# Two transformer blocks on one core: both ends of the kernel rebuilt

## The chip, the cores and the metric

The kernel runs on 1 core of one Trainium2 chip. The metric is the device time of one execution in microseconds (us). Three runs of the kernel before gave 2267.41, 2269.45 and 2269.79 us; the median is 2269.45 us. All numbers below are from these runs and from one execution of the same kernel taken by the profiler.

## The reference

Two blocks follow each other on 256 tokens of width 2048, all in float32. What matters here is how the computation begins and how it ends:

```python
mem_n = rms_norm(mem, norm_mem_g)                    # mem: 256 x 2048
mkv = mem_n @ w_mem_kv                               # 2048 x 2048: the first products of the kernel
h = rms_norm(x, norm_in_g); proj = h @ w_in          # and so on: three kinds of attention, gates, w_out
...                                                  # second block: LRU, retention, w_out_2
u = rmsnorm(h, ln2_w)
ff = silu(u @ w_ffn_gate) * (u @ w_ffn_up)           # d_ff = 5632
h = h + ff @ w_ffn_down                              # 5632 x 2048: the last products
return rmsnorm(h, final_norm_w)                      # a mean over the whole row, then a scale
```

The last norm needs the sum of squares of a token's whole row of 2048 numbers before any number of that row can be written.

## The kernel before

**Weights.** Each product of 256 tokens with a weight is cut into tiles of 512 output columns and each tile into chunks of 256 rows of the weight (`per` = 2 blocks of 128), 512 KB each. A chunk is loaded by SyncE's (SP's) queue into one of four slots of `raw`. ScalarE (ACT, `split`, L509) rounds it to `w_hi`, VectorE (DVE, `split`, L743) makes the rest `w_lo` = raw - `w_hi`. A float32 product is three products of such parts: for each block of 128 rows and each of the two token halves `t`, TensorE (PE) does hi x hi (L1283), hi x lo (L1284) and lo x hi (L1285). A chunk is 2 x 2 x 3 = 12 matmuls. The first weight, `w_mem_kv`, has 8 chunks in a tile; the last, `w_ffn_down`, has 22. The tokens' side must be ready in both parts too (`memT_hi`, `memT_lo`).

**Order.** ACT, DVE and PE each run a list written out by hand: in `run(tile)` they go through the tile's chunks, and behind chunk `h` they do what hooks say. ACT and DVE work strictly in this order, so a hook that waits holds back the `split` of the next chunk.

**The start.** SP loads `ident` and the vectors (L430 to L432), then the first quarter of `mem`, the first chunk of weight, and the other quarters and chunks in turn; then, behind the first tile, the tables (704 KB) and `x` (two loads of 1 MB). PE turns the vectors (L1321, L1322) into `cols`. A quarter q of `mem` is turned by `job(q)`: 8 transposes on PE (L1150), 4 copies with a factor on ACT (`job_hi`, L540), 4 operations on DVE (`job_lo`, L780). PE does job(0) and job(1) before chunk 0, job(2) behind chunk 0 and job(3) behind chunk 1. ACT and DVE do job 0 first, job 1 behind their split of chunk 0, job 2 behind that of chunk 2, job 3 behind that of chunk 3. Chunks 2q and 2q+1 need job q.

**The end.** The last tile of `w_ffn_down` closes columns 1536 to 2047. Then DVE adds both token halves (L949), ACT squares both (L526), DVE multiplies both by the norm's weight (L1046), sums up (L773), makes the mean (L750); GpSimd (POOL) takes the power -0.5 (L461); DVE scales half 0 (L1137) and ACT scales half 1 (L725), each in two pieces of 1024 columns; SP stores four pieces of 512 KB (L450) and waits for them.

Of the kernel before, what the change touches and what calls it, by code (L numbers as in the profile page):

```python
# [112 lines left out]
def build(nc, x, mem, w_in, w_mkv, w_pa, w_pb, w_pm, w_out, fin1_g, w_in2, w_out2, w_gate, w_up, w_down,  # L113
          fin2_g, gate_a, gate_x, vecs, consts_d, decay_d, spill, out):
    ctx = ExitStack()
    with ctx:
# [100 lines left out]
        def bank(b, lo=0, hi=NW):  # L217
# [26 lines left out]
            sem(n) for n in ("in_const", "in_vec", "in_res", "in_g1", "in_dec", "in_gw", "in_g2"))  # L244
        spilled, in_h2, stored = sem("spilled"), sem("in_h2"), sem("stored")
        x_added = sem("x_added")
        pool_c, vec_ps, cols_ready, lam_abs, lam_e, lam_ready = (
            sem(n) for n in ("pool_c", "vec_ps", "cols_ready", "lam_abs", "lam_e", "lam_ready"))

# [154 lines left out]
        @block.sync  # L404
        def _(sp):
            w = Walk()

            def load(tile, then={}):
                per = tile.get("per", 2)
                src = tile["w"].rearrange("(c p) n -> p c n", p=P)  # L410
                if w.loop:
                    sp.to_reg(tile["col"] * 4)
                for h in chunks(tile):
                    s = w.n["g"] % SLOTS
                    sp.wait_ge(lo_ready, w("g", 1))
# [18 lines left out]
            first, *rest = tiles_memkv()  # L434
            load(first, {0: lambda: load_mem(1), 1: lambda: load_mem(2), 2: lambda: load_mem(3)})
            sp.dma_start(consts[:, C_ID + P:], consts_d[:, C_ID + P:]).then_inc(in_tables, 16)
            for t in range(NT):
                sp.dma_start(x_tok[:, t], x[t * P:(t + 1) * P, :]).then_inc(in_x[t], 16)
            load_all(rest + tiles_attention() + tiles_merge(0))
            w.rounds(sp, NG - 1, lambda i: load_all(tiles_merge(i + 1)))  # L440
            w.rounds(sp, NG // 2, lambda i: load_all(res_tiles(w_out, "m", None, i)))
            load_all(tiles_two())
            load_all(tiles_out2())
            w.rounds(sp, NF, lambda i: load_all(tiles_ffn(i)))
            w.rounds(sp, NG // 2, lambda i: load_all(res_tiles(w_down, "ff", None, i, FC // 2)))
            for t in range(NT):
                for m in range(2):
                    sp.wait_ge(out_made[t], m + 1)
                    c = slice(m * D // 2, (m + 1) * D // 2)
                    sp.dma_start(out[t * P:(t + 1) * P, c], h2[:, t, c]).then_inc(stored, 16)  # L450
            sp.wait_ge(stored, 32 * NT)


        @block.gpsimd
        def _(pool):
            nc.gpsimd.memset(mneg_c[:, :], -0.5).then_inc(pool_c, 1)
            pool.wait_ge(pool_c, 1)

            def norm_root(k, dst):
                pool.wait_ge(n_mean, k + 1)  # L460
# [36 lines left out]
            norm_root(5, R["out"]["r"])  # L497


        @block.scalar  # L500
        def _(act):
# [181 lines left out]
            def log_sigmoid_exp():  # L683
# [7 lines left out]
            four[1]["act_hooks"] = {7: [lambda: squares(x_tok, sumsq_x, lambda t: act.wait_ge(in_x[t], 16))]}  # L691
# [27 lines left out]
            act.wait_ge(x_added, 1)  # L719
            tile_squares(prev)  # L720
            act.wait_ge(out_scaled, NG)
            act.wait_ge(n_root, 6)
            for m in range(2):
                c = slice(m * D // 2, (m + 1) * D // 2)
                nc.scalar.activation(h2[:, 1, c], h2[:, 1, c], ACT.Copy, scale=R["out"]["r"][:, 1:2]).then_inc(out_made[1], 1)  # L725


        @block.vector
        def _(dve):
# [349 lines left out]
            def last_factors(name, k):  # L1079
# [11 lines left out]
            four[0]["dve_hooks"] = {0: jobs(memT_hi, memT_lo, V_MEM, 1), 2: jobs(memT_hi, memT_lo, V_MEM, 2),  # L1091
                                    3: jobs(memT_hi, memT_lo, V_MEM, 3), 7: [mem_factors]}
# [4 lines left out]
            job_lo(0, memT_hi, memT_lo, cols[:, V_MEM:V_MEM + KC])  # L1097
            prev = chain(four, None)
            log_sigmoid()
            tiles = tiles_attention()  # L1100
# [32 lines left out]
            sum_up(sums_a[:, :, :])
            root(sum_ab, 5)
            for m in range(2):
                c = slice(m * D // 2, (m + 1) * D // 2)
                nc.vector.tensor_scalar(h2[:, 0, c], h2[:, 0, c], R["out"]["r"][:, 0:1], None, ALU.mult).then_inc(out_made[0], 1)  # L1137


        @block.tensor  # L1140
        def _(pe):
# [11 lines left out]
            def job(q, src, arrived):  # L1153

                pair = q % 2
                for s in arrived:
                    pe.wait_ge(s, 16)
# [108 lines left out]
            def run(tile, prev):  # L1266
# [6 lines left out]
                for i, h in enumerate(chunks(tile)):  # L1273
                    s = w.n["g"] % SLOTS
                    for f in need.get(h, ()):
                        f()
                    pe.wait_ge(lo_ready, w("g", SLOTS + 1))
                    for k in range(per):
                        kc = h * per + k
                        first, last = kc == 0, kc == hcs * per - 1  # L1280
                        for t in range(NT):
                            x_hi, x_lo = (m[:, k0 + kc, t * P:(t + 1) * P] for m in (hi, lo))
# [16 lines left out]
                        ret_y(tile["ret"])  # L1299
                    for f in hooks.get(i, ()):  # L1300
                        f()
                return tile

            def chain(tiles, prev):
# [2 lines left out]
                    prev = run(tile, prev if tile.get("follow", True) else None)  # L1307
                return prev

            def begin(tile, src, in_):  # L1310

                for q in range(QUAD):
                    quads[q] = w.n[f"j{q % 2}"] + q // 2 + 1
                for q in range(2):
                    job(q, src, [in_[q]])
                tile["pe_hooks"] = {q - 2: [lambda q=q: job(q, src, [in_[q]])] for q in (2, 3)}
                tile["need"] = {2 * q: [lambda q=q: parts_ready(q)] for q in range(QUAD)}
# [48 lines left out]
            prev = ffn_last(NF - 1)  # L1366
            for k in range(NG // 2):
                tiles = res_tiles(w_down, "ff", h2, k, FC // 2, "out")
                if k == 0:
                    tiles[0]["need"] = {0: [quads_ready], FC // 2 - 2: [quads_ready]}  # L1370
                prev = chain(tiles, prev)
# [61 lines left out]
```

## Time and profile before

| | before |
|---|---|
| median of 3 runs | 2269.45 us |
| span of the profiled execution | 2267.3 us |
| first matmul of the weights starts | 14.34 us |
| last matmul starts | 2254.26 us |
| TensorE busy in the span | 98% |
| mean granted clock | 0.995 |

The page gives the profiled execution as its span, from the first to the last instruction; it prints no other time of its own, so the span is its own time, and the median of the runs lies 2.15 us above it. "Busy" of TensorE is the time in which a matmul is under way; a matmul's duration (0.39 us) is longer than the distance to the next one, since they are pipelined. "[2.47 <-DVE w_lo L743]" behind a row means that the engine stood idle for 2.47 us before it and that this instruction let it go on.

### The profile page before, as it was taken

Reading aid. Unit: us, or ns where it says so; the run is one execution under the profiler, and the core shown is the slowest. Engines: PE = TensorE matmul, PEld = TensorE weight load, DVE = VectorE, ACT = ScalarE, POOL = GpSimd, SP = SyncE. Lnnn points to the kernel's source line nnn. Section 1 sums busy time; section 2 is a strip of 40 time slices with the busy share of each in tenths; the row PEclk is TensorE's granted clock in tenths of the full one; section 3 lists DMA queues with packets and bytes.
Section 4 is the critical chain, followed back from the end, with each engine's and each line's share of the span. In section 5 each row is a group of like instructions: output and inputs, shape, how many; then the busy total and the mean of one; then the engine's idle time right before and its main releaser. Section 6 shows DMA issues by size and latency. Waiting matters only on the chain.

```text
span 2267.3 us, 26426 instructions
## 1 busy us (share of the span) xinstructions
PE 2227.8 (98%) x10222; PEld 1849.5 (82%) x10222; DVE 1273.5 (56%) x1541; ACT 1019.5 (45%) x1224; POOL 17.0 (1%) x30
## 2 busy tenths in 40 slices
PE   8999999999999999999999999999999999999997
PEld 6888888888888788888888887778888888888886
DVE  4555556565454545545666888555555555554443
ACT  5534444444443444444544655354444444444443
POOL 0000000000000000000000000000000000000000
PEclk9999999999999999999999999999999999999999
DMA  7565455556654656567565554556666666666663
GB/s 266 158 209 164 157 184 167 160 185 186 195 160 128 186 177 205 183 213 267 187 222 177 186 160 157 186 181 182 195 191 188 186 192 187 192 205 195 193 193 134
DMA packets 213104, 421.66 MB, mean 186 GB/s; under 512 B 12808, under 2 KB 13072, under 8 KB 211600
## 3 DMA queue, kind: packets, MB, share of 16 engines
q1 hardware_dynamic: 211424, 409.85, 58.5%
q0 software_dynamic: 1584, 10.49, 1.2%
q8 instruction: 65, 1.06, 0.2%
q14 instruction: 31, 0.25, 0.0%
HBM read 416.09 MB, written 4.19 MB: 185 GB/s over the span
## 4 chain that ended last, share of the span: by engine, by line
PE 82%; issue 11%; DVE 4%; DMA 1%; ACT 1%; POOL 0%; ACTq 0%; SPq 0%; POOLq 0%; DVEq 0%
PE ps L1283 26%; PE ps L1285 26%; PE ps L1284 26%; PE ps L1150 2%; DVE w_lo L743 1%; PE ps L1180 1%; PE ps L1202 1%; ACT w_hi L509 0%; DMA raw<-in_w_mem_kv 0%; DMA raw<-in_w_out 0%; PE ps L1191 0%; DVE lt_a L870 0%; DMA mem_tok<-in_mem 0%; DMA raw<-in_w_in 0%; DVE memT_lo L780 0%
## 5 line engine op out<-in xcount | busy, mean ns | idle before, releaser
L743 DVE TENSOR_TENSOR w_lo<-raw,w_hi 128x1024 fp32r<-128x1024 f32 (+1 forms) x776 | 933.8, 1213 | 784.2 <-ACT w_hi L509 782.1
L509 ACT ACTIVATE w_hi<-raw 128x1024 fp32r<-128x1024 f32 (+1 forms) x776 | 809.8, 1051 | 909.5 <-PE ps L1285 850.1
L1283 PE MATMUL ps<-w_hi,xT_hi 128*128 128x512 f32 x1088 | 430.7, 396 | 1.3 <-DVE w_lo L743 1.3
L1285 PE MATMUL ps<-w_hi,xT_lo 128*128 128x512 f32 x1088 | 424.4, 390 | 0.0
L1284 PE MATMUL ps<-w_lo,xT_hi 128*128 128x512 f32 x1088 | 423.7, 389 | 0.0
L1283 PE MATMUL ps<-w_hi,u2T_hi 128*128 128x512 f32 x704 | 274.9, 390 | 0.0
L1285 PE MATMUL ps<-w_hi,u2T_lo 128*128 128x512 f32 x704 | 274.0, 389 | 0.0
L1284 PE MATMUL ps<-w_lo,u2T_hi 128*128 128x512 f32 x704 | 273.9, 389 | 0.0
L1285 PEld LDWEIGHTS ps<-w_hi,xT_lo 128*128 128x128 f32 x1088 | 204.2, 188 | 43.3
L1283 PEld LDWEIGHTS ps<-w_hi,xT_hi 128*128 128x128 f32 x1088 | 204.4, 188 | 42.9 <-issue 1.7
L1284 PEld LDWEIGHTS ps<-w_lo,xT_hi 128*128 128x128 f32 x1088 | 204.5, 188 | 40.8
L1283 PE MATMUL ps<-w_hi,uT_hi 128*128 128x512 f32 x384 | 153.4, 399 | 1.7 <-DVE w_lo L743 1.7
L1285 PEld LDWEIGHTS ps<-w_hi,u2T_lo 128*128 128x128 f32 x704 | 132.2, 188 | 27.5
L1284 PEld LDWEIGHTS ps<-w_lo,u2T_hi 128*128 128x128 f32 x704 | 132.2, 188 | 27.1
L1283 PEld LDWEIGHTS ps<-w_hi,u2T_hi 128*128 128x128 f32 x704 | 132.2, 188 | 27.1
L1285 PE MATMUL ps<-w_hi,uT_lo 128*128 128x512 f32 x384 | 149.9, 390 | 0.0
L1284 PE MATMUL ps<-w_lo,uT_hi 128*128 128x512 f32 x384 | 149.5, 389 | 0.0
L1283 PE MATMUL ps<-w_hi,ffT_hi 128*128 128x512 f32 x352 | 137.0, 389 | 0.0
L1285 PE MATMUL ps<-w_hi,ffT_lo 128*128 128x512 f32 x352 | 137.0, 389 | 0.0
L1284 PE MATMUL ps<-w_lo,ffT_hi 128*128 128x512 f32 x352 | 136.9, 389 | 0.0
L1283 PEld LDWEIGHTS ps<-w_hi,uT_hi 128*128 128x128 f32 x384 | 72.1, 188 | 17.0 <-issue 2.9
L1285 PEld LDWEIGHTS ps<-w_hi,uT_lo 128*128 128x128 f32 x384 | 72.1, 188 | 15.5
(225 smaller groups left out, 2138.4 us busy)
## 6 DMA issues: line engine op xcount, KB each, us to landing
raw<-in_w_in SPq DMA_DIRECT2D x368, 512.0 KB, 4.3
raw<-in_w_ffn_gate SPq DMA_DIRECT2D x88, 512.0 KB, 4.5
raw<-in_w_ffn_up SPq DMA_DIRECT2D x88, 512.0 KB, 4.4
raw<-in_w_ffn_down SPq DMA_DIRECT2D x88, 512.0 KB, 4.7
raw<-in_w_out SPq DMA_DIRECT2D x64, 512.0 KB, 4.6
raw<-in_w_mem_kv SPq DMA_DIRECT2D x32, 512.0 KB, 5.1
raw<-in_w_proj_m SPq DMA_DIRECT2D x16, 512.0 KB, 3.8
raw<-in_w_proj_a SPq DMA_DIRECT2D x16, 512.0 KB, 4.2
```

What stands on the lines that cost most here:

```text
L509: nc.scalar.activation(w_hi[:, s, 0:per], raw[:, s, 0:per], ACT.Copy).then_inc(hi_ready, 1)
L743: nc.vector.tensor_tensor(w_lo[:, s, 0:per], raw[:, s, 0:per], w_hi[:, s, 0:per].bitcast(F32), ALU.subtract)\
L1150: ins = nc.tensor.transpose(ps[:, o:o + P], src(t, c), ident)
L1180: ins = nc.tensor.matmul(ps[:, o:o + P], qT[:, qc, t * P:(t + 1) * P], kT[:, kc, kt * P:(kt + 1) * P], start=n == 0, stop=n == len(qs) - 1)
L1202: ins = nc.tensor.matmul(ps[:, o:o + width], probsT[:, a + n * P:a + (n + 1) * P], v(kt), start=n == 0, stop=n == len(blocks) - 1)
L1283: nc.tensor.matmul(bank(2 * par + t), x_hi, w_hi[:, s, k], start=first, stop=False)
L1284: nc.tensor.matmul(bank(2 * par + t), x_hi, w_lo[:, s, k], start=False, stop=False)
L1285: ins = nc.tensor.matmul(bank(2 * par + t), x_lo, w_hi[:, s, k], start=False, stop=last)
```

## The change

At the start: `ident` and the vectors are loaded by ACT's queue, `mem`'s first quarter is the first load of SP's. A small ACT copy (of POOL's constant) stands ahead of ACT's first wait for PE. The first quarter of `mem` is turned in two halves, with the first chunk's matmuls in another order: the 8 that need no `w_lo`, then job(1), then the 4 with `w_lo` (`open_tile`). PE does 8 and 6 transposes of `ident` whose output nobody reads (`warm`). PE's job(2) now stands behind chunk 1 and job(3) behind chunk 3. `x` is loaded in 8 pieces of 256 KB during the second tile, ahead of the tables. At the end: the last four chunks (a slot each) are done for token half 0 first and then for half 1 (`by_rows`), and each half is closed, scaled and stored by itself, in pieces of 512 columns, by SP's and ACT's queues.

```diff
@@ sync
-            sp.dma_start(ident, consts_d[:, C_ID:C_ID + P]).then_inc(in_const, 16)
-            sp.dma_start(vec_a[:, :], vecs[0:P]).then_inc(in_vec, 16)
-            sp.dma_start(vec_b[0:V_END - P, :], vecs[P:V_END]).then_inc(in_vec, 16)
             load_mem(0)
-            load(first, {0: lambda: load_mem(1), 1: lambda: load_mem(2), 2: lambda: load_mem(3)})
+            load(first, {0: lambda: load_mem(1), 2: lambda: load_mem(2), 3: lambda: load_mem(3)})
+            load(second, {h: lambda h=h: load_x(h // QUAD, h % QUAD) for h in range(NT * QUAD)})
...
@@ scalar, start (act_hooks of the first tile stay {0: job 1, 2: job 2, 3: job 3, 5: squares of mem})
+            act.dma_start(ident, ...); act.dma_start(vec_a[:, :], ...); act.dma_start(vec_b[0:V_END - P, :], ...)
+            act.wait_ge(pool_c, 1)
+            nc.scalar.activation(mneg_c[:, :], mneg_c[:, :], ACT.Copy, scale=0.5).then_inc(pool_c, 1)
             act.wait_ge(cols_ready, 1)
-            job_hi(0, memT_hi, cols[:, V_MEM:V_MEM + KC])
+            act.wait_ge(t0_done, 1)
+            for c in range(2): ... memT_hi[:, c] ...      # then t0_hi
+            four[0]["act_hooks"][0].insert(0, second_half)  # c = 2, 3, ahead of job 1; the same on DVE
...
@@ scalar, end
+            for t in range(NT):
+                act.wait_ge(rows_added, t + 1)
+                nc.scalar.activation(sq_out[...], h2[:, t, cs], ACT.Square, accum_out=sums_b[:, t, 0:1])
+                act.wait_ge(rows_root, t + 1)
+                for m in range(2, NG):
+                    ... ACT.Copy of 512 columns with r[t] ..., then act.dma_start(out[t * P:(t + 1) * P, c], ...)
@@ vector, end
+            link(nc.vector.reduce_sum(sum_ab, sums_a[:, :, 0:NG - 1], AX))   # the first three tiles, ahead of the end
+            for t in range(NT):
+                dve.wait_ge(acc_done, t + 1)
+                add of 512 columns (rows_added); mean of one column (rows_mean); times g_row2, 512 columns (out_scaled)
+                dve.wait_ge(rows_root, t + 1)
+                for m in range(2): ... scale of 512 columns ... .then_inc(rows_scaled, 1)   # SP stores these
@@ tensor
+                by_rows = SLOTS if tile.get("by_rows") else 0
+                for i, h in enumerate(chunks(tile)[:hcs - by_rows]): ...
+                if by_rows:
+                    for t in range(NT):
+                        for c in range(SLOTS): ... the 6 matmuls of chunk c for half t ...
+                        ins.then_inc(acc_done, 1)
+            def open_tile(tile):
+                pe.wait_ge(hi_ready, 1)
+                ... 8 matmuls: x_hi and x_lo with w_hi[:, 0, k] ...
+                job(1, mem_tok, [in_mem[1]])
+                pe.wait_ge(lo_ready, SLOTS + 1)
+                ... 4 matmuls: x_hi with w_lo[:, 0, k] ...
             def begin(tile, src, in_):
-                for q in range(2): job(q, src, [in_[q]])
-                tile["pe_hooks"] = {q - 2: [lambda q=q: job(q, src, [in_[q]])] for q in (2, 3)}
+                pe.wait_ge(in_[0], 16)
+                4 transposes (t0_done), 4 transposes (tx_done[0])
+                warm(6)
+                tile["opens"] = open_tile
+                tile["pe_hooks"] = {2 * q - 3: [lambda q=q: job(q, src, [in_[q]])] for q in (2, 3)}
...
+            warm(8)        # behind the transposes of the vectors
```

## Rows read from the trace of the kernel before

**Rows 1.** The page, part 1: busy time, share of the span, instructions.
```profile
PE 2227.8 (98%) x10222; PEld 1849.5 (82%) x10222; DVE 1273.5 (56%) x1541; ACT 1019.5 (45%) x1224; POOL 17.0 (1%) x30
```

**Rows 2.** Chain of waits, first 10 us: start, length, what (us).
```profile
2.08 4.24 DMA mem_tok<-in_mem
6.37 1.98 PE ps L1150 x8
8.42 1.28 ACT L540
```

**Rows 3.** Timeline of PE, chunks 0, 2, 8: start, us, engine, line, operation.
```profile
14.34 0.77 PE L1283 MATMUL ps<-w_hi,memT_hi 128*128 128x512 f32 x1 [2.47 <-DVE w_lo L743]
...
18.59 1.03 PE L1150 MATMUL ps<-consts,mem_tok 128*128 128x128 f32 x8
...
23.00 0.47 PE L1283 MATMUL ps<-w_hi,memT_hi 128*128 128x512 f32 x1
...
40.17 0.50 PE L1283 MATMUL ps<-w_hi,memT_hi 128*128 128x512 f32 x1 [0.56 <-DVE w_lo L743]
```

**Rows 4.** Timeline of SP, PE and ACT in the first 13 us.
```profile
0.76 0.39 SPq L430 DMA_DIRECT2D consts<-in_consts  x1
3.40 0.45 PE L1321 MATMUL ps<-consts,vec_a 128*128 128x128 f32 x1 [3.40 <-DMA vec_b<-in_vectors]
9.72 1.57 ACT L540 ACTIVATE memT_hi<-ps,cols 128x256 fp32r<-128x256 f32 x4
11.16 1.07 ACT L509 ACTIVATE w_hi<-raw 128x1024 fp32r<-128x1024 f32 x1
```

**Rows 5.** Timeline around 1475 us, a job whose result PE waits for.
```profile
1472.97 1.03 PE L1150 MATMUL ps<-consts,h 128*128 128x128 f32 x8
...
1475.65 1.66 DVE L973 SCALAR_TENSOR_TENSOR u2T_lo<-ps,cols,u2T_hi 128x256 fp32r<-128x256 f32 x4 [3.92 <-ACT u2T_hi L630]
1478.58 0.76 PE L1283 MATMUL ps<-w_hi,y2T_hi 128*128 128x512 f32 x1 [4.58 <-DVE w_lo L743]
```

**Rows 6.** Timeline of PE: other pauses and what followed.
```profile
112.21 0.47 PE L1283 MATMUL ps<-w_hi,xT_hi 128*128 128x512 f32 x1 [1.01 <-DVE w_lo L743]
727.52 2.18 PE L1191 MATMUL ps<-consts,scores 128*128 128x128 f32 x9 [2.18 <-ACT scores L550]
```

**Rows 7.** Windows: us, busy and instructions per engine, PEclk, DMA share, GB/s.
```profile
730.00:731.00 1.00, 1.00 (x4) 0.78 (x3) 0.00 (x0) 0.93 (x2) 0.00 (x0) 0.62 0.00 0
1479.00:1481.00 2.00, 2.00 (x6) 1.52 (x6) 2.00 (x3) 0.40 (x1) 0.00 (x0) 0.50 0.66 163
```

**Rows 8.** Timeline of the end, all engines.
```profile
2244.95 1.23 DVE L743 TENSOR_TENSOR w_lo<-raw,w_hi 128x1024 fp32r<-128x1024 f32 x1 [1.49 <-ACT w_hi L509]
...
2254.26 0.39 PE L1285 MATMUL ps<-w_hi,ffT_lo 128*128 128x512 f32 x1
2254.68 1.28 DVE L949 TENSOR_TENSOR h<-h,ps 128x512 f32<-128x512 f32 x2 [8.50 <-PE ps L1285]
2256.00 0.63 ACT L526 ACTIVATE sq_out<-h 128x512 bf16<-128x512 f32 x1 [11.08 <-DVE h L949]
...
2257.36 1.29 DVE L1046 TENSOR_TENSOR h<-h,g_row 128x512 f32<-128x512 f32 x2 [1.40 <-ACT sq_out L526]
...
2259.03 0.71 POOL L461 TENSOR_TENSOR small<-small,mneg_c 128x2 f32<-128x2 f32 x1 [243.80 <-DVE small L750]
...
2259.84 2.19 ACT L725 ACTIVATE h<-h,small 128x1024 f32<-128x1024 f32 x2 [2.50 <-POOL small L461]
2260.56 2.79 SPq L450 DMA_DIRECT2D out_dram<-h  x4
```

**Rows 9.** Windows of the end, columns as in rows 7.
```profile
2260.00:2262.00 2.00, 0.00 (x0) 0.00 (x0) 1.19 (x2) 2.00 (x2) 0.00 (x0) 0.50 0.31 127
2262.00:2266.00 4.00, 0.00 (x0) 0.00 (x0) 0.00 (x0) 0.02 (x1) 0.00 (x0) 0.50 1.03 421
```

**Rows 10.** Waits and tile view of the output's stores.
```profile
DMA to landing us min/median/max: 2.6/3.7/4.7
```

More of the change, by code:

```diff
@@ L246, in build @@
         x_added = sem("x_added")
+        t0_done, t0_hi, t0_lo = (sem(n) for n in ("t0_done", "t0_hi", "t0_lo"))
+        acc_done, rows_added, rows_sq, rows_mean, rows_root, rows_scaled = (
+            sem(n) for n in ("acc_done", "rows_added", "rows_sq", "rows_mean", "rows_root", "rows_scaled"))
         pool_c, vec_ps, cols_ready, lam_abs, lam_e, lam_ready = (
@@ L428, in load_mem, with load_x @@
                 sp.dma_start(mem_tok[:, :, c], mem.rearrange("(t p) n -> p t n", p=P)[:, :, c]).then_inc(in_mem[q], 16)
-            sp.dma_start(ident, consts_d[:, C_ID:C_ID + P]).then_inc(in_const, 16)
-            sp.dma_start(vec_a[:, :], vecs[0:P]).then_inc(in_vec, 16)
-            sp.dma_start(vec_b[0:V_END - P, :], vecs[P:V_END]).then_inc(in_vec, 16)
+            def load_x(t, q):
+                c = slice(q * NW, (q + 1) * NW)
+                sp.dma_start(x_tok[:, t, c], x[t * P:(t + 1) * P, c]).then_inc(in_x[t], 16)
             load_mem(0)
-            first, *rest = tiles_memkv()
-            load(first, {0: lambda: load_mem(1), 1: lambda: load_mem(2), 2: lambda: load_mem(3)})
+            first, second, *rest = tiles_memkv()
+            load(first, {0: lambda: load_mem(1), 2: lambda: load_mem(2), 3: lambda: load_mem(3)})
+            load(second, {h: lambda h=h: load_x(h // QUAD, h % QUAD) for h in range(NT * QUAD)})
             sp.dma_start(consts[:, C_ID + P:], consts_d[:, C_ID + P:]).then_inc(in_tables, 16)
-            for t in range(NT):
-                sp.dma_start(x_tok[:, t], x[t * P:(t + 1) * P, :]).then_inc(in_x[t], 16)
             load_all(rest + tiles_attention() + tiles_merge(0))
@@ L690, in _ @@
                                     5: [mem_in, lambda: squares(mem_tok, sumsq_m, lambda t: None)]}
-            four[1]["act_hooks"] = {7: [lambda: squares(x_tok, sumsq_x, lambda t: act.wait_ge(in_x[t], 16))]}
+            four[1]["act_hooks"] = {7: [lambda: squares(x_tok, sumsq_x, lambda t: act.wait_ge(in_x[t], 16 * QUAD))]}
             for n in (2, 3):
@@ L695, in _, with second_half @@
             four[3]["act_hooks"][5] = [log_sigmoid_exp]
-            act.wait_ge(cols_ready, 1)
-            job_hi(0, memT_hi, cols[:, V_MEM:V_MEM + KC])
+            act.dma_start(ident, consts_d[:, C_ID:C_ID + P]).then_inc(in_const, 16)
+            act.dma_start(vec_a[:, :], vecs[0:P]).then_inc(in_vec, 16)
+            act.dma_start(vec_b[0:V_END - P, :], vecs[P:V_END]).then_inc(in_vec, 16)
+            act.wait_ge(pool_c, 1)
+            nc.scalar.activation(mneg_c[:, :], mneg_c[:, :], ACT.Copy, scale=0.5).then_inc(pool_c, 1)
+            act.wait_ge(cols_ready, 1)
+            act.wait_ge(t0_done, 1)
+            for c in range(2):
+                ins = nc.scalar.activation(memT_hi[:, c], bank(4, c * S, (c + 1) * S), ACT.Copy, scale=cols[:, V_MEM + c:V_MEM + c + 1])
+            ins.then_inc(t0_hi, 1)
+            def second_half():
+                act.wait_ge(tx_done[0], 1)
+                for c in range(2, QUAD):
+                    ins = nc.scalar.activation(memT_hi[:, c], bank(4, c * S, (c + 1) * S), ACT.Copy,
+                                               scale=cols[:, V_MEM + c:V_MEM + c + 1])
+                ins.then_inc(tx_hi[0], 1)
+                w.step("j0", "h0")
+            four[0]["act_hooks"][0].insert(0, second_half)
             prev = chain(four, None)
@@ L718, in _ @@
                 prev = chain(res_tiles(w_down, "ff", h2, k, FC // 2, "out"), prev)
[L719 to L725, printed above, removed]
+            cs = slice((NG - 1) * NW, NG * NW)
+            for t in range(NT):
+                act.wait_ge(rows_added, t + 1)
+                nc.scalar.activation(sq_out[:, t * NW:(t + 1) * NW], h2[:, t, cs], ACT.Square,
+                                     accum_out=sums_b[:, t, 0:1]).then_inc(rows_sq, 1)
+                act.wait_ge(rows_root, t + 1)
+                for m in range(2, NG):
+                    c = slice(m * NW, (m + 1) * NW)
+                    if m == NG - 1:
+                        act.wait_ge(out_scaled, NG + t)
+                    nc.scalar.activation(h2[:, t, c], h2[:, t, c], ACT.Copy, scale=R["out"]["r"][:, t:t + 1]).then_inc(out_made[t], 1)
+                    act.wait_ge(out_made[t], m - 1)
+                    act.dma_start(out[t * P:(t + 1) * P, c], h2[:, t, c]).then_inc(stored, 16)
         @block.vector
@@ L1090, in _, with first_lo, second_half @@
             four = tiles_memkv()
-            four[0]["dve_hooks"] = {0: jobs(memT_hi, memT_lo, V_MEM, 1), 2: jobs(memT_hi, memT_lo, V_MEM, 2),
+            def first_lo(hi_made, some, lo_made):
+                dve.wait_ge(hi_made, 1)
+                for c in some:
+                    ins = nc.vector.scalar_tensor_tensor(memT_lo[:, c], bank(4, c * S, (c + 1) * S), cols[:, V_MEM + c:V_MEM + c + 1],
+                                                         memT_hi[:, c].bitcast(F32), ALU.mult, ALU.subtract)
+                ins.then_inc(lo_made, 1)
+            def second_half():
+                first_lo(tx_hi[0], range(2, QUAD), tx_free[0])
+                w.step("j0", "h0")
+            four[0]["dve_hooks"] = {0: [second_half] + jobs(memT_hi, memT_lo, V_MEM, 1), 2: jobs(memT_hi, memT_lo, V_MEM, 2),
                                     3: jobs(memT_hi, memT_lo, V_MEM, 3), 7: [mem_factors]}
@@ L1096, in _ @@
             four[2]["dve_hooks"][1] = [x_factors]
-            job_lo(0, memT_hi, memT_lo, cols[:, V_MEM:V_MEM + KC])
+            first_lo(t0_hi, range(2), t0_lo)
             prev = chain(four, None)
@@ L1128, in _ @@
                 prev = chain(res_tiles(w_down, "ff", h2, k, FC // 2, "out"), prev)
-            post(prev, 0, x_added)
-            w.step("sq")
-            scale_out(NG - 1)
             dve.wait_ge(sq_done, w.n["sq"])
[L1133 to L1137, printed above, removed]
+            link(nc.vector.reduce_sum(sum_ab, sums_a[:, :, 0:NG - 1], AX))
+            link(nc.vector.tensor_scalar(sum_ab, sum_ab, 1.0 / D, EPS, ALU.mult, ALU.add))
+            par, cs = prev["par"], slice((NG - 1) * NW, NG * NW)
+            for t in range(NT):
+                dve.wait_ge(acc_done, t + 1)
+                nc.vector.tensor_tensor(h2[:, t, cs], h2[:, t, cs], bank(2 * par + t), ALU.add).then_inc(rows_added, 1)
+                dve.wait_ge(rows_sq, t + 1)
+                nc.vector.tensor_scalar(meansq[:, t:t + 1], sums_b[:, t, 0:1], 1.0 / D, sum_ab[:, t:t + 1],
+                                        ALU.mult, ALU.add).then_inc(rows_mean, 1)
+                nc.vector.tensor_tensor(h2[:, t, cs], h2[:, t, cs], g_row2[:, cs], ALU.mult).then_inc(out_scaled, 1)
+                dve.wait_ge(rows_root, t + 1)
+                for m in range(2):
+                    c = slice(m * NW, (m + 1) * NW)
+                    nc.vector.tensor_scalar(h2[:, t, c], h2[:, t, c], R["out"]["r"][:, t:t + 1], None, ALU.mult).then_inc(rows_scaled, 1)
         @block.tensor
@@ L1272, in run @@
                 at_ = (0, 1, 2, 3) if hcs == 4 else (0, 2, 4, 5)
-                for i, h in enumerate(chunks(tile)):
+                by_rows = SLOTS if tile.get("by_rows") else 0
+                for i, h in enumerate(chunks(tile)[:hcs - by_rows]):
                     s = w.n["g"] % SLOTS
@@ L1276, in run @@
                         f()
+                    if tile.get("opens") and h == 0:
+                        ins = tile["opens"](tile)
                     pe.wait_ge(lo_ready, w("g", SLOTS + 1))
@@ L1281, in run @@
                         for t in range(NT):
+                            if tile.get("opens") and h == 0:
+                                continue
                             x_hi, x_lo = (m[:, k0 + kc, t * P:(t + 1) * P] for m in (hi, lo))
@@ L1301, in run @@
                         f()
+                if by_rows:
+                    for t in range(NT):
+                        for c in range(SLOTS):
+                            s = (w.n["g"] + c) % SLOTS
+                            if t == 0:
+                                pe.wait_ge(lo_ready, w("g", SLOTS + 1 + c))
+                            for k in range(per):
+                                kc = (hcs - SLOTS + c) * per + k
+                                last = kc == hcs * per - 1
+                                x_hi, x_lo = (m[:, k0 + kc, t * P:(t + 1) * P] for m in (hi, lo))
+                                nc.tensor.matmul(bank(2 * par + t), x_hi, w_hi[:, s, k], start=False, stop=False)
+                                nc.tensor.matmul(bank(2 * par + t), x_hi, w_lo[:, s, k], start=False, stop=False)
+                                ins = nc.tensor.matmul(bank(2 * par + t), x_lo, w_hi[:, s, k], start=False, stop=last)
+                        ins.then_inc(acc_done, 1)
                 return tile
@@ L1308, in chain, with warm @@
                 return prev
+            def warm(n):
+                for _ in range(n):
+                    nc.tensor.transpose(bank(7, 0, P), ident, ident)
+            def open_tile(tile):
+                hi, lo = PARTS[tile["x"]]
+                pe.wait_ge(hi_ready, 1)
+                for k in range(2):
+                    for t in range(NT):
+                        x_hi, x_lo = (m[:, k, t * P:(t + 1) * P] for m in (hi, lo))
+                        nc.tensor.matmul(bank(t), x_hi, w_hi[:, 0, k], start=k == 0, stop=False)
+                        nc.tensor.matmul(bank(t), x_lo, w_hi[:, 0, k], start=False, stop=False)
+                job(1, mem_tok, [in_mem[1]])
+                pe.wait_ge(lo_ready, SLOTS + 1)
+                for k in range(2):
+                    for t in range(NT):
+                        ins = nc.tensor.matmul(bank(t), hi[:, k, t * P:(t + 1) * P], w_lo[:, 0, k], start=False, stop=False)
+                return ins
             def begin(tile, src, in_):
@@ L1313, in begin @@
                     quads[q] = w.n[f"j{q % 2}"] + q // 2 + 1
-                for q in range(2):
-                    job(q, src, [in_[q]])
-                tile["pe_hooks"] = {q - 2: [lambda q=q: job(q, src, [in_[q]])] for q in (2, 3)}
-                tile["need"] = {2 * q: [lambda q=q: parts_ready(q)] for q in range(QUAD)}
+                pe.wait_ge(in_[0], 16)
+                transposes(lambda t, c: src[:, t, c * P:(c + 1) * P], 4 * NW, 2).then_inc(t0_done, 1)
+                transposes(lambda t, c: src[:, t, (2 + c) * P:(3 + c) * P], 5 * NW, 2).then_inc(tx_done[0], 1)
+                w.step("j0", "h0")
+                warm(6)
+                tile["opens"] = open_tile
+                tile["pe_hooks"] = {2 * q - 3: [lambda q=q: job(q, src, [in_[q]])] for q in (2, 3)}
+                tile["need"] = {1: [lambda: parts_ready(0)], 0: [lambda: pe.wait_ge(t0_lo, 1)],
+                                **{2 * q: [lambda q=q: parts_ready(q)] for q in range(1, QUAD)}}
             pe.wait_ge(in_const, 16)
@@ L1368, in _ @@
                 tiles = res_tiles(w_down, "ff", h2, k, FC // 2, "out")
+                tiles[1]["by_rows"] = k == NG // 2 - 1
                 if k == 0:
```

15 lines of the change are left out of this document (8 added, 7 removed).

## Prediction, made before the change was run

> **What bounds the kernel now.** I read the page first: TensorE is busy for 98% of the span [rows 1], so in the middle nothing but PE counts, and each microsecond by which PE's stream of matmuls starts later, pauses or ends later moves the whole. That leaves the two ends. The chain of waits over the first 15 us [rows 2] shows what holds the first matmul back until 14.34: the first quarter of `mem` lands at 6.3, then 8 transposes and a table load of 1.28 us on ACT, and behind them the copies, DVE's lows and `w_lo`. The timelines [rows 3, 4] give the chunk times, that of the end [rows 8] the serial chain behind the last matmul: it starts at 2254.26 and ends at 2254.65, so 12.65 us of the span lie behind it. Then I looked in the middle for places like those that the change makes [rows 5 to 7].
>
> **Reference times of the start before.** Chunk 0 takes 14.34 to 18.59, 4.25 us for its 12 matmuls, chunk 2 starts at 23.00, chunk 8 at 40.17 after a pause of 0.56 [rows 3]. The matmul before that pause could have been followed about 0.16 earlier than its modelled end of 39.61, at 39.45; chunks 2 to 7 thus took 16.45 us, 2.74 each. Chunk 0 at the low level (1.2 GHz, its first matmul 0.77) is 1.5 us dearer than a chunk at the high one (2.4 GHz). Chunk 4 started at 23.00 + 2 x 2.74 = 28.5.
>
> **Start, the gain.** `mem`'s first quarter is issued at 0.76 instead of 2.08 [rows 2, 4]; with the same 4.24 to landing it is there at 5.0. `ident` and the vectors, from ACT's queue at about the same 0.76, are turned at 3.4 as before; 8 idle transposes at the rate of rows 2 (8 in 1.98) end at about 5.9, 0.9 later than the landing. 4 transposes, 1.0: 6.9. The table load falls away from the path, since the small copy fetches it while PE waits. ACT: two copies (1.57 / 4 each) 0.8, `w_hi` 1.07 [rows 4]: 8.8. DVE's two lows fit beside it. First matmul at 8.9 instead of 14.34, 5.4 earlier. Bounds: 8.0 if the copies find `w_hi`'s data early and the warm-up costs nothing, 10.5 if the shared DMA engines delay the small loads and `mem`.
>
> **Start, what it adds.** This is the step that decides. PE's job(2) moved from behind chunk 0 to behind chunk 1 and job(3) from behind chunk 1 to behind chunk 3, job(1) into chunk 0; the hooks of ACT and DVE stayed where they were. ACT splits chunk 1 only after job 1, chunk 3 only after job 2, chunk 4 only after job 3. What PE then waits for is: 8 transposes, 4 copies on ACT, 4 lows on DVE, `w_lo` on DVE. Before, PE had issued each job two chunks or more ahead, so the row of waits was covered. The trace has this very sequence uncovered once: from the first transpose of a job at 1472.97 to the next matmul at 1478.58 are 5.6 us [rows 5], which hold 1.03 of transposes, the copies (1.57, rows 4), 1.66 of lows and a `w_lo` (1.23, rows 8). So:
> - chunk 0: 8 matmuls from 8.9, 1.9: 10.8; job(1) and its sequence 5.6: chunk 1 starts at 16.4. The 4 matmuls with `w_lo` lie inside; PE stands still for 3.8.
> - chunk 1 with a low clock 4.25: 20.65; job(2) and its sequence: chunk 3 starts at 26.25. Chunk 2 lies inside; pause 1.9.
> - chunk 3 2.74: 29.0; job(3) and its sequence, with nothing beside it: chunk 4 at 34.6; pause 4.6.
>
> Chunk 4 starts 34.6 - 28.5 = 6.1 us later than before, although the first matmul is 5.4 earlier. In these pauses I let the clock fall: after the pause of 4.58 us it stood at 0.50, the low level, and the first matmul took 0.76; after that of 2.47 the first took 0.77; after that of 2.18 the clock was still low 2.5 us on; after one of 1.01 the first took only 0.47 [rows 3, 5 to 7]. A fall costs 1.5 us. I count it after the first pause (in the 4.25 above) and after the third (+1.5), not after the 1.9. Back comes the stall before chunk 8, 40.17 - 39.45 = 0.7: that was data, with tables and x (2.7 MB) on the queue in one block, now 256 KB behind each chunk. Sum of the start: 6.1 + 1.5 - 0.7 = +6.9. Bounds: +3.8 if neither of the two falls happens, +8.5 if the 1.9 us pause brings one as well; the first matmul's bounds add -0.9 or +1.6.
>
> **Do the idle transposes raise the clock?** At 727.52 PE came back from a pause with 9 transposes (2.18 us) and then matmuls; in 730 to 731 the mean clock was 0.62, so it rose there, some 3.2 us after PE came back, of which transposes took 1.8 to 2.2 [rows 6, 7]. In chunk 0, matmuls alone, 1.5 us lost at half speed means 3 us at the low level [rows 3]: as long. So transposes seem to count, and 3.4 to 8.9, filled with them, should leave the clock high for the 8 matmuls; I take 1.9 us for them.
> The Trainium skill, page "TensorE: Matmul & The Clock Gate", Part 4: PE-mode transpose, says otherwise: the full clock is not engaged by transposes, which don't count as busy in the same way. By the page the warm-up would bring nothing.
> What it would cost here is 8 matmuls at the low level, 1.5 us more, with the later steps shifted by as much: a rival below.
>
> **End, what it removes.** The last four chunks' matmuls are the same 48; half 0 closes 24 matmuls earlier, 5.4 us, and its add, square, root, scale and stores fit under half 1's matmuls. `w_lo` of the last chunk is ready at 2246.2 [rows 8], and half 0 reaches it three quarters into its 5.4 us from 2243.8 on, at 2247.9, so no wait there. Behind the last matmul remain, for half 1, with durations of rows 8: add 0.7 (half of 1.28, and start), square with its read of the sum 0.75, mean 0.25, root 0.71 and 0.1: root at +2.6 instead of +5.2. Its multiplication by `g_row2` (0.65) lies beside the root. Then DVE's first 512 columns are ready at +3.0 and SP issues; ACT's pieces take 0.6 each with an issue (0.45 as the middle one of SP's, up to 1.1) between: the last store is issued at +4.4. Before, 2 MB moved at 421 GB/s from 2261.4, 0.85 after the first issue, until 2266.4 [rows 8, 9], the stores being the bound. Now it is 1 MB: from +3.85, 2.5 us: +6.4, landing 0.5 later, then 0.35 until the span's end: +7.3 instead of +12.65. Gain 5.4. Bounds: 4.0 (two slow issues on ACT, 1.1 each, as one of SP's four was), 6.2 (only the last 256 KB's own way from +4.4, with 2.6 less 0.6 to landing [rows 10]).
>
> **Sum.** 2267.3 + 6.9 - 5.4 = 2268.8 for the profiled execution; the median of the runs lies 2.15 above the span, so 2271. This is no change: what a measurement of this kernel can tell from none is about 0.2%, 4.5 us.
>
> **Rivals.**
> - A, the jobs aren't exposed: ACT and DVE get past the hooks in time, and PE keeps its lead. Start -5.4 - 0.7, end -5.4: 2269.45 - 11.5 = 2258. For it speaks that all of the loads are earlier; against it, that the order of instructions on ACT and DVE leaves no way round and that rows 5 show the price. Chance 0.1.
> - B, the clock stays high over the pauses: start +3.8, 2268. For it speaks only that the trace has few pauses of this length; the three above speak against. 0.12.
> - C, on the other side: the clock. Where PE isn't fed by matmuls it goes low: the warm-up does nothing (+1.5) and the pause of 1.9 us, too, ends low (+1.5). 2271 + 3 = 2274. It decides, just past the bound of what can be told, where a pause shorter than 2.18 us is enough and the transposes bring nothing. Both halves: 0.13. The first half alone, idle transposes that bring nothing, gives 2272.5; it has 0.15 of the likeliest case's chance below.
> This first half is the Trainium skill's rule of the page named above, followed here.
> - D, the second queue: packets of `mem`, the first chunk and the small loads share the engines, and PE's first transposes come 1.6 us later: 2272.6. 0.08.
> - My forecast, with its neighbours of one half of C: 0.57 in all; its own range 2267 to 2274.
>
> **How the numbers follow.** Predicted 2271. The range goes from 2264.5 (B with a better end) to 2275.5 (C with the short end); outside are A and a little at the top. Faster than 2265: A 0.1 and 0.05 of B. Slower than 2274: half of C, and the forecast with both bounds bad, 0.2. Within 0.2%: 0.65.
>
> **What would show it.** First weight matmul at 8 to 10.5. Three pauses of PE before the rows of `w_lo` of chunks 1, 3 and 4, near 3.8, 1.9 and 4.6, and PEclk 0.50 behind the first and the third. Chunk 8 at about 47 instead of 40.2. The last matmul about 7 us later than 2254.3, and 7.3 us from its end to the end of the span. I am wrong if PE has no pause over 1 us between the first matmul and 40 us (A), or if the end takes over 9 us.

## Result and profile after: slower by a quarter of a percent

| | before | after |
|---|---|---|
| median of 8 runs | 2269.9 us | 2275.72 us |
| lowest, highest | 2267.41, 2270.78 | 2273.29, 2276.33 |
| span of the profiled execution | 2267.3 us | 2274.3 us |
| first matmul of the weights | 14.34 | 12.15 |
| last matmul starts | 2254.26 | 2265.77 |

The median before is now that of 8 runs, 2269.9 instead of 2269.45. The ratio is 1.0024, 95% interval 1.0015 to 1.0033: slower, clear of the noise though small. The profiled execution of the changed kernel is one of its slower ones (the spans of its 8 runs go from 2271.3 to 2274.4), so the spans differ by 7.0 us and the medians by 5.8. 2271 (range 2264.5 to 2275.5) had been predicted. The two ends went opposite ways, as in the prediction's sum, but the start lost more than it was charged with.

The timeline of TensorE over the first 40 us of the changed kernel answers to [rows 3, 4]. L1379 is the idle transposes, L1197 the transposes of `mem`, L1388 and L1394 chunk 0, L1335 the later chunks. The columns are start, us, engine, line, operation, and in brackets the idle time before and what ended it:

```profile
6.77 0.45 PE L1413 MATMUL ps<-consts,vec_a 128*128 128x128 f32 x1 [6.77 <-DMA vec_b<-in_vectors]
7.35 1.97 PE L1379 MATMUL ps<-consts 128*128 128x128 f32 x8
9.11 1.45 PE L1197 MATMUL ps<-consts,mem_tok 128*128 128x128 f32 x8
10.39 0.82 PE L1379 MATMUL ps<-consts 128*128 128x128 f32 x6
12.15 0.47 PE L1388 MATMUL ps<-w_hi,memT_hi 128*128 128x512 f32 x1 [0.94 <-DVE memT_lo L1124]
...
14.07 1.03 PE L1197 MATMUL ps<-consts,mem_tok 128*128 128x128 f32 x8
14.87 1.17 PE L1394 MATMUL ps<-w_lo,memT_hi 128*128 128x512 f32 x4
19.68 0.47 PE L1335 MATMUL ps<-w_hi,memT_hi 128*128 128x512 f32 x1 [3.65 <-DVE w_lo L772]
...
24.10 1.03 PE L1197 MATMUL ps<-consts,mem_tok 128*128 128x128 f32 x8
...
29.62 0.50 PE L1335 MATMUL ps<-w_hi,memT_hi 128*128 128x512 f32 x1 [1.72 <-DVE w_lo L772]
...
32.48 1.04 PE L1197 MATMUL ps<-consts,mem_tok 128*128 128x128 f32 x8
38.10 0.77 PE L1335 MATMUL ps<-w_hi,memT_hi 128*128 128x512 f32 x1 [4.58 <-DVE w_lo L772]
```

The reader is to see three pauses (3.65, 1.72 and 4.58 us) where the kernel before had none, each behind a job of 8 transposes, and a first row that waits for the vectors until 6.77 instead of 3.40. The chain of waits names what lies in the last pause, the same members as in [rows 5]. Such a sequence, from a job's first transpose to the matmul that waits for its result, is called the row of waits below:

```profile
33.93 1.20 ACT memT_hi L545 x3
35.13 0.02 issue
35.16 1.66 DVE memT_lo L809 x4
36.82 1.14 DVE w_lo L772
37.96 0.14 issue
38.10 0.77 PE ps L1335
```

And the windows (us, busy and instructions of PE, PEld, DVE, ACT, POOL, then PEclk, DMA share, GB/s) show the clock low behind the first and the third pause:

```profile
20.00:21.00 1.00, 1.00 (x4) 0.84 (x3) 0.67 (x1) 0.00 (x0) 0.00 (x0) 0.59 0.21 78
...
38.00:44.00 6.00, 5.90 (x14) 4.68 (x15) 3.17 (x3) 5.15 (x7) 0.00 (x0) 0.50 0.76 254
```

The end, which answers to [rows 8], half 1 alone behind the last matmul (it ends at 2266.16):

```profile
2265.77 0.39 PE L1366 MATMUL ps<-w_hi,ffT_lo 128*128 128x512 f32 x1
2266.20 0.69 DVE L1176 TENSOR_TENSOR h<-h,ps 128x512 f32<-128x512 f32 x1 [1.72 <-PE ps L1366]
2266.92 0.63 ACT L745 ACTIVATE sq_out<-h 128x512 bf16<-128x512 f32 x1 [1.44 <-DVE h L1176]
...
2267.97 0.94 POOL L502 TENSOR_TENSOR small<-small,mneg_c 128x1 f32<-128x1 f32 x1 [4.41 <-DVE small L1178]
2268.94 0.72 ACT L752 ACTIVATE h<-h,small 128x512 f32<-128x512 f32 x1 [1.29 <-POOL small L502]
...
2269.45 0.81 SPq L453 DMA_DIRECT2D out_dram<-h  x2
...
2270.82 0.34 ACTq L754 DMA_DIRECT2D out_dram<-h  x1
```

From 2266.16 to 2274.3 are 8.1 us, against 12.65 before. So -4.5 at the end, and +11.5 at the start (2265.77 - 2254.26).

### The profile page after: what moved, and what is told of

The parts are those of the page before. It is cut to its first block, busy times and chain, and to the rows that moved or that the text cites. A ratio compares the mean times of both kernels' runs of the same rounds, so it can differ in the third digit from the quotient of the medians.

```text
span 2274.3 us, 26472 instructions
## 1 busy us (share of the span) xinstructions
PE 2232.0 (98%) x10236; PEld 1852.8 (81%) x10236; DVE 1274.2 (56%) x1545; ACT 1020.4 (45%) x1227; POOL 18.1 (1%) x31
## 4 chain that ended last, share of the span: by engine, by line
PE 93%; DVE 4%; ACT 1%; DMA 1%; issue 1%; POOL 0%; ACTq 0%; POOLq 0%; DVEq 0%
PE ps L1335 29%; PE ps L1337 29%; PE ps L1336 29%; PE ps L1197 2%; DVE w_lo L772 2%; PE ps L1227 1%; PE ps L1249 1%; DMA raw<-in_w_out 0%; ACT w_hi L514 0%; PE ps L1238 0%; DVE lt_a L899 0%; DVE memT_lo L809 0%; DMA vec_b<-in_vectors 0%; ACT memT_hi L545 0%; DVE y_tok L868 0%
## 5 line engine op out<-in xcount | busy, mean ns | idle before, releaser
L1335 PE MATMUL ps<-w_hi,xT_hi 128*128 128x512 f32 x1088 | 430.7, 396 | 1.3 <-DVE w_lo L772 1.3
L1335 PE MATMUL ps<-w_hi,u2T_hi 128*128 128x512 f32 x704 | 274.9, 390 | 0.0
L1335 PEld LDWEIGHTS ps<-w_hi,xT_hi 128*128 128x128 f32 x1088 | 204.4, 188 | 42.8 <-issue 1.7
L1335 PE MATMUL ps<-w_hi,uT_hi 128*128 128x512 f32 x384 | 153.4, 399 | 1.7 <-DVE w_lo L772 1.7
L1335 PEld LDWEIGHTS ps<-w_hi,u2T_hi 128*128 128x128 f32 x704 | 132.2, 188 | 27.0
L1335 PE MATMUL ps<-w_hi,ffT_hi 128*128 128x512 f32 x336 | 130.8, 389 | 0.0
L1337 PE MATMUL ps<-w_hi,ffT_lo 128*128 128x512 f32 x336 | 130.7, 389 | 0.0
L1336 PE MATMUL ps<-w_lo,ffT_hi 128*128 128x512 f32 x336 | 130.7, 389 | 0.0
L1335 PEld LDWEIGHTS ps<-w_hi,uT_hi 128*128 128x128 f32 x384 | 72.2, 188 | 16.9 <-issue 2.8
```

## Experiments

The theory was that PE's moved jobs leave the row of waits (transposes, copies, lows, `w_lo`) uncovered, so that PE stands still for it. Its rivals were that the loads of `mem` or of the weights hold PE wherever the jobs stand; that the loss is in the middle or at the end; and that it takes the other edits to make it hurt.

**1. The jobs back, the rest of the change kept.**

```diff
-                tile["pe_hooks"] = {2 * q - 3: [lambda q=q: job(q, src, [in_[q]])] for q in (2, 3)}
+                tile["pe_hooks"] = {q - 2: [lambda q=q: job(q, src, [in_[q]])] for q in (2, 3)}
```

> The changed kernel with one edit: TensorE's job(2) stands behind chunk 0 and job(3) behind chunk 1 again, as before the change; the hooks of ScalarE and VectorE are not touched. Theory (the moved jobs expose the row transposes, copies, lows, w_lo): the pauses of 1.72 and 4.58 us ahead of chunks 3 and 4 are gone, the first one of 3.65 stays, since job(1) isn't moved, and chunk 4 runs at the high clock, which gives back some 2.5 to 3 us more. Span 1.7 + 4.6 + 2.6 = 9 us under the changed kernel's 2274.3, near 2265, about 5 us faster than before. Rival (the late loads of mem hold TensorE, wherever the jobs stand): new pauses of 2 us or more before job(2) and job(3), and a span over 2270.

Measured: 2263.97 us, ratio to before 0.9976 (0.9966 to 0.9985), span 2262.0. One line turns a loss of 0.24% into a gain of 0.24%. Two pauses are gone, and job(2) and job(3) wait for nothing. The timeline of PE:

```profile
15.89 1.04 PE L1197 MATMUL ps<-consts,mem_tok 128*128 128x128 f32 x8
19.70 0.47 PE L1335 MATMUL ps<-w_hi,memT_hi 128*128 128x512 f32 x1 [2.77 <-DVE w_lo L772]
22.55 1.03 PE L1197 MATMUL ps<-consts,mem_tok 128*128 128x128 f32 x8
50.64 1.04 PE L1197 MATMUL ps<-consts,stage 128*128 128x128 f32 x8
```

The rival (late loads of mem) falls. The span came out 3 us lower than expected. 1.6 us of that is the clock, which did not fall behind the first pause either: chunk 1's 12 matmuls take 19.70 to 22.55, 2.85 us against 4.42 in the changed kernel. Another 0.8 is job(2) itself, which now lies inside that pause (2.77 instead of 3.65) and no longer behind chunk 1.

**2. The jobs moved, in the kernel before, nothing else.**

```diff
-                tile["pe_hooks"] = {q - 2: [lambda q=q: job(q, src, [in_[q]])] for q in (2, 3)}
+                tile["pe_hooks"] = {2 * q - 3: [lambda q=q: job(q, src, [in_[q]])] for q in (2, 3)}
```

> The kernel before with one edit alone: TensorE's job(2) behind chunk 1 and job(3) behind chunk 3. Theory (this step alone makes the row of waits uncovered): chunk 3 starts at 27.0 after a pause of 1.8, chunk 4 at 35.3 after one of 4.6 instead of at 28.5, then 1.5 to 2.9 us at the low clock, and the stall of 0.7 before chunk 8 is gone: span 7.6 to 9 us over 2267.3, near 2275.5 (1.0036). Rival (it hurts only together with the other edits of the start): under 3 us.

Measured: 2277.95 us, ratio 1.0038 (1.0024 to 1.0052), span 2276.1, 8.8 over before. The two pauses stand where they were expected:

```profile
27.05 0.50 PE L1283 MATMUL ps<-w_hi,memT_hi 128*128 128x512 f32 x1 [1.74 <-DVE w_lo L743]
29.95 1.03 PE L1150 MATMUL ps<-consts,mem_tok 128*128 128x128 f32 x8
35.56 0.77 PE L1283 MATMUL ps<-w_hi,memT_hi 128*128 128x512 f32 x1 [4.57 <-DVE w_lo L743]
```

With the first experiment this shows the cause from both sides: the one line is enough to lose 8.8 us of span (7.9 between the medians), and without it the change gains.

**3. Each end alone.** Edits: the kernel before with only the end's hunks of the diff, and with only the start's.

> The kernel before with only the change's end (last four chunks by token halves, output in 512 columns on two queues). Theory (the end alone gains and nothing of it touches the start): 8.1 us from the last matmul's end to the span's end instead of 12.65, span 2262.8, 4.5 us under the kernel before (0.998). Rival (part of the loss of the changed kernel is in the order by halves, by waits for w_lo or dearer matmuls in the last 48): the last four chunks take over 11.2 us, and the gain is under 3 us.

> The kernel before with only the change's start (loads, halves of the first quarter, idle transposes, moved jobs, x in 8 pieces). Theory (all of the loss is at the start): span 11.5 us over the kernel before, 2278.8 (1.005), with the three pauses of 3.65, 1.7 and 4.6 us and chunk 8 at about 51.9 instead of 40.2. Rival (part of the shift arises later, in the middle): chunk 8 at the same place, but a span that differs from 2267.3 plus that shift by more than 1 us.

Measured: end alone 2266.02 us, ratio 0.9983 (0.9973 to 0.9992), span 2263.2, of which 8.2 behind the last matmul (start 2254.60); start alone 2280.43 us, ratio 1.0047 (1.003 to 1.0064), span 2278.0. The end gains some 4 and the start loses 10.7; together -4.1 and +10.7 make +6.6, the changed kernel's span moved by +7.0. The half order costs nothing: the last 48 matmuls take 10.65 us from the first start to the last, 10.66 before. In the start alone the three pauses are 3.65, 1.72 and 4.57; its last matmul starts 0.9 us earlier than the changed kernel's, since the clock came back sooner behind the third.

**4. The small loads ahead of mem, on one queue.**

```diff
-            act.dma_start(ident, ...); act.dma_start(vec_a[:, :], ...); act.dma_start(vec_b[0:V_END - P, :], ...)
+            sp.dma_start(ident, ...); sp.dma_start(vec_a[:, :], ...); sp.dma_start(vec_b[0:V_END - P, :], ...)   # ahead of load_mem(0)
```

> The changed kernel with one edit: ident and the two vector loads are issued by SyncE ahead of mem's first quarter, as before the change, and ScalarE issues no load. Theory (small loads on a second queue wait for the big transfers' packets on the same engines, and vec_b lands at 6.77 instead of 3.40 us): vec_b lands at 3.4 again, the 8 idle transposes end at 5.9, mem's first quarter lands at 6.3, the first matmul of the weights starts at 9.3 to 9.8 instead of 12.15, and the span falls by 2.5 to 3 us to about 2271.6. The three pauses stay. Rival (the late vectors cost nothing, mem's landing sets the first matmul): the first matmul stays within 0.5 us of 12.15 and so does the span of 2274.3.

Measured: 2273.37 us, ratio to before 1.0014 (1.0004 to 1.0024), span 2272.2. The timeline of PE: the vectors are there at 3.44, mem's first quarter at 6.28, and the first matmul of the weights starts at 9.43.

```profile
3.44 0.45 PE L1413 MATMUL ps<-consts,vec_a 128*128 128x128 f32 x1 [3.44 <-DMA vec_b<-in_vectors]
4.02 1.97 PE L1379 MATMUL ps<-consts 128*128 128x128 f32 x8
6.28 1.97 PE L1197 MATMUL ps<-consts,mem_tok 128*128 128x128 f32 x8 [0.29 <-DMA mem_tok<-in_mem]
```

So `vec_b`, 4 KB issued at 1.76 on the second queue, let PE start 5.0 us after its issue beside the large transfers, and 1.7 us after it when it went ahead of them. The edit changes the queue and the order together, and the small loads alone on ACT's queue were not run. That ACT's queue is slow by itself is unlikely: at the end of the changed kernel none of the 8 stores of 256 KB, 4 of them issued on it, took over 3.4 us to land, and from 3 to 7 us the windows show the core's 16 DMA engines busy for 90% or more of the time. Of the 2.7 us that the first matmul gained, 2.1 reached the span; the interval of the ratio overlaps that of the changed kernel, so this size rests on the traces.

**5. x in pieces.** In the kernel before, `x` in 8 loads of 256 KB behind the second tile's chunks, ahead of the tables.

> The kernel before with x loaded in 8 pieces of 256 KB behind the chunks of the second tile, ahead of the tables, and nothing else. Theory (tables and x in one block of 2.7 MB made the weights late): the pause of 0.56 us before chunk 8 is gone, chunk 8 starts at 39.4 to 39.5 instead of 40.17, and the span is 0.7 us lower, 2266.6. Rival (the stall has another cause, as the 3.9 us of squares on ScalarE ahead of chunk 6): the pause stays at 0.5 to 0.6.

Measured: no pause before chunk 8, which starts at 39.78 and not at 39.4 to 39.5, since chunk 2 had already started at 23.37 instead of 23.00; the transposes in the next tile at 50.66 instead of 51.19; span 2266.7; ratio 0.9994 (0.9984 to 1.0004), too little for the runs to tell. The trace bears out the term of 0.7, by its pause.

**6. Without the idle transposes, in the changed kernel.** Edit: both calls of `warm` removed.

> The changed kernel without the 14 idle transposes. Theory (the transposes of ident both raise the clock and hold TensorE up, since the first 8 come between the vectors and mem's first quarter, which landed long ago): mem's transposes start at 7.4 instead of 9.1, the first matmul at 10.4 instead of 12.15, but its first 5 to 8 matmuls go at 0.43 instead of 0.23 each, 1.0 to 1.6 us lost; span 0 to 1 us under 2274.3. Rival (idle transposes do nothing to the clock): all 8 matmuls at the high level as with them, span 1.75 us lower.

Measured: 2275.3 us, ratio 1.0028 (1.0016 to 1.0041), span 2273.1. The first matmul starts at 10.50 and all 8 go at the low level, until 14.05; chunk 4 starts at 36.86 instead of 38.10. The idle transposes did both: they raised the clock, and they stood in the way by 1.65 us. At chunk 1 the two nearly cancel (19.68 with them, 20.00 without). Chunk 4 is earlier because the clock did not fall behind the first pause here: chunk 1 took 2.85 us and not 4.42. The medians of the runs can't tell this kernel from the changed one (1.0028 against 1.0024).

**7. All three rows covered.** The edits of 1 and 4, and job 1 on ACT and DVE one chunk later:

```diff
-            four[0]["act_hooks"] = {0: jobs(memT_hi, V_MEM, 1), 2: ...
+            four[0]["act_hooks"] = {0: [], 1: jobs(memT_hi, V_MEM, 1), 2: ...      # and the same for dve_hooks
```

> Three edits to the changed kernel: the small loads ahead of mem on SyncE; TensorE's job(2) behind chunk 0 and job(3) behind chunk 1; and ScalarE's and VectorE's job 1 behind their split of chunk 1 instead of chunk 0, so that w_lo of chunk 1 does not wait for it. Theory (every one of the three pauses was a row transposes, copies, lows, w_lo standing uncovered): no pause over 1 us from the first matmul at 9.4 to the end, chunk 4 starts near 23.4 (28.5 in the kernel before), the end is 8.1 long: span about 2257, 10 us under the kernel before (0.9955). Rival (the data is the next limit: the weights' transfers, issued when w_lo is made, can't keep up with a start 5 us earlier): the pauses come back as waits for raw, over 2 us in sum, and the span is over 2259.

> The same kernel without any of the 14 idle transposes. Theory (idle transposes raise the clock, but here TensorE is at real transposes from 6.3 on anyway): the first matmul stays at 9.3, the low level lasts 0 to 3 us longer, and the span is 0 to 1.5 us over the one with them. Rival (transposes don't count): no difference at all in which matmuls are at the low level.

Measured: with the idle transposes 2257.55 us, ratio 0.9951 (0.9934 to 0.9967), span 2255.7; without them 2260.77 us, ratio 0.9962 (0.9948 to 0.9976), span 2259.1. The best kernel of this study is 11.7 us under before and 18 under the change. Job 1's new place has no run of its own; the trace shows only that the first pause (2.77 in experiment 1) is gone with it. In the timeline of PE of the first no row has a pause between the first matmul and the next tile's job at 45.5:

```profile
8.38 1.49 PE L1379 MATMUL ps<-consts 128*128 128x128 f32 x6
11.97 1.03 PE L1197 MATMUL ps<-consts,mem_tok 128*128 128x128 f32 x8
12.76 1.17 PE L1394 MATMUL ps<-w_lo,memT_hi 128*128 128x512 f32 x4
13.77 1.03 PE L1197 MATMUL ps<-consts,mem_tok 128*128 128x128 f32 x8
17.39 1.04 PE L1197 MATMUL ps<-consts,mem_tok 128*128 128x128 f32 x8
45.51 1.03 PE L1197 MATMUL ps<-consts,stage 128*128 128x128 f32 x8
```

Without the idle transposes the low level lasts over the 8 first matmuls (9.65 to 13.20) and job(1), and chunk 1 starts at 16.83 instead of 14.56: 2.3 us, where 0 to 1.5 were expected. The other 1.1 of the spans' 3.4 arose later and is not shown to come from the idle transposes: behind a pause of 2.18 us near 722, the same in both, the clock fell without them and stayed high with them. The intervals of the two ratios overlap, but each of the 4 runs with them (2257.38 to 2258.44) is under each of the 5 without (2259.73 to 2261.14).

**8. Another cut of the end.** The kernel of 7, with DVE scaling 1536 columns of half 1 and ACT 512.

> The kernel with three edits, and for token half 1 VectorE scales 1536 of the 2048 columns and ScalarE 512, instead of 1024 each. Theory (the end is now a chain of short steps, and its last store waits for ScalarE's second piece: 0.72 + 0.36 + 0.72): the last store is issued 0.5 us earlier and the span's end with it, 7.6 instead of 8.1 us behind the last matmul. Rival (the 1 MB of the stores, 2.5 us at 420 GB/s, is the bound): no change over 0.2 us.

Measured: 2258.83 us, ratio 0.9953 (0.9936 to 0.9969). From the end of the last matmul (2248.91) to that of the span (2256.9) are 8.0 us, against 8.2 (2247.50 to 2255.7): the rival holds. The last store is issued 4.2 us behind the last matmul's end (2253.1) instead of 4.7 (2252.16), and yet the end moved by 0.2 only. The stores' transfer is what ends last, not the issue of the last one. In the windows (columns as above), 2 us of stores at 385 GB/s:

```profile
2253.00:2255.00 2.00, 0.00 (x0) 0.00 (x0) 0.00 (x0) 0.00 (x0) 0.00 (x0) 0.50 1.03 385
```

## Why the prediction was right, and where it was short

- **The row of waits: right.** The steps predicted starts of 8.9, 16.4, 26.25 and 34.6 for the first matmul and chunks 1, 3 and 4; measured 12.15, 19.68, 29.62 and 38.10. From the first matmul on that is 7.5, 17.35, 25.7 against 7.5, 17.5, 25.95. Pauses 3.8, 1.9, 4.6 against 3.65, 1.72, 4.58. A sequence taken from 1475 us, another weight and another stage, held to 0.3 us. Experiments 1 and 2 show that it is the cause of the second and the third pause; the first is gone in experiment 7.
- **The step that failed: "`ident` and the vectors, from ACT's queue at about the same 0.76, are turned at 3.4 as before".** They were turned at 6.77. Rival D had this mechanism with 1.6 us and a chance of 0.08; the first matmul came 3.25 us after the 8.9 predicted, beyond even the bound of 10.5, and experiment 4 gives back 2.7 of it. These transfers went ahead of the large ones before the change and stand beside them after it, so their landing had to be priced anew.
- **"A fall costs 1.5 us": right in kind, wrong in size for the third.** Chunk 1 took 4.4 us (19.68 to 24.10) where 4.25 was predicted. But behind the third pause the low level lasted 6 us, over 14 matmuls, and cost 2.9; in experiment 2, with the same pause, 6 us too, in the start alone 3.5 us. One measured instance gave a single price for what varies between these runs.
- **The stall of 0.7: right** (experiment 5).
- **Idle transposes raise the clock: right.** In the changed kernel 8 idle transposes took 1.97 and then 6 of them 0.82, before any matmul of the weights had run, so transposes alone brought the high level. Without them the first 8 matmuls were at the low one (experiment 6). It is not sure in every run: in the first kernel of experiment 7 the same 14 left the first matmul at the low level (0.77, at 9.76), in that of experiment 8 at the high one (0.47, at 9.71). The Trainium skill's rule ("TensorE: Matmul & The Clock Gate", Part 4: PE-mode transpose), by which they don't, disagrees with these float32 transposes, and the measurement decides.
- **The end: -5.4 predicted, -4.5 measured.** Three terms were mis-sized by 0.3 us each. The chain to the first store: the root is there 2.8 behind the last matmul's end and not 2.6 (POOL's power of one column took 0.94, that of two 0.71), and SP's first store is issued at +3.3 and not +3.0. The transfer: by windows of 0.5 us it moved from about +4.1 to +6.9, 2.8 us and not 2.5, at 328 to 401 GB/s in its full windows, where 421 had been taken. The tail behind it: 1.2 and not 0.85. That an ACT piece of 512 columns took 0.72 and not 0.6 changed nothing (experiment 8). Half 0 was hidden, as said.
- **The sum.** Start +6.9 predicted: the small loads' 3.25 and the clock's 1.4 more make +11.5, the end 0.9 less. All errors pointed one way. The median, 2275.7, lies 0.2 beyond the top of the range; as a ratio, 1.0024, it lies just inside (2275.5 / 2269.45 is 1.0027). That much agreement is luck: the top of the range came from C, and neither of C's halves happened, since the idle transposes worked and the clock stayed high behind the pause of 1.72 (0.50 for the next matmul, 0.39 after it). The range's lower end was too low by its own terms: B's 2268 with a better end (0.8) and the earlier first matmul (0.9) gives 2266.3, not 2264.5. Slower than 2274 was given 0.2, within 0.2% 0.65; it is slower by 0.24%.

## What to carry to other kernels

Where engines run lists written by hand, a step moved on one engine has to be followed on the others: a hook that waits stands ahead of work that the first engine needs next, and its whole row of waits (here 5.6 us) shows unless enough other work lies between: one chunk of 2.7 us left 1.7 us bare. Find one place in the trace where that row is already bare and use it as the price. Where a tiny load gates everything, issue it ahead of the large ones rather than beside them on another queue.

## What the runs showed of the hardware

- A second queue did not protect a small transfer: 4 KB took 5.0 us from its issue until PE could go on beside 512 KB transfers of the other queue, 1.7 us when issued ahead of them (experiment 4).
- The length of a pause does not settle whether the clock falls. Behind the pause of 2.18 us near 722 it stayed high in the first kernel of experiment 7 and fell in that of experiment 8 (from 722.99 on, for 6 matmuls). There PE was 0.2 us ahead before this place and is 1.4 us behind at the next pause. Rows of experiment 7, then of experiment 8:

```profile
724.28 0.40 PE L1335 MATMUL ps<-w_hi,yT_hi 128*128 128x512 f32 x1
733.60 0.47 PE L1335 MATMUL ps<-w_hi,yT_hi 128*128 128x512 f32 x1 [2.77 <-DVE w_lo L772]
```

```profile
724.42 0.63 PE L1335 MATMUL ps<-w_hi,yT_hi 128*128 128x512 f32 x1
735.01 0.47 PE L1335 MATMUL ps<-w_hi,yT_hi 128*128 128x512 f32 x1 [2.77 <-DVE w_lo L772]
```

- The first matmul behind a pause does not settle it either. In experiment 6 it took 0.47 behind 3.64 us, and all 12 of chunk 1 stayed high, until 22.85; in the changed kernel it took 0.47 behind 3.65 us, the next 0.46, and those from 20.24 on 0.63:

```profile
20.00 0.47 PE L1335 MATMUL ps<-w_hi,memT_hi 128*128 128x512 f32 x1 [3.64 <-DVE w_lo L772]
```

- The low level, once there, lasted 3 us (experiment 4, from 17.41) to 6 us (the changed kernel, from 38.10) of dense matmuls behind the pauses of the start. So a pause of this kind cost 0 to 3 us on top of itself, and this can hide effects of the size studied here: experiments 7 and 8 have the same start to 0.2 us (45.51 and 45.36) and last matmuls at 2247.11 and 2248.52. What decides it is not shown.
